# First panel by row parts, split-operand query jobs, and a new order of work in three mixers of a two-block transformer kernel

## What is computed

```python
# first block: three branches, then a mixture of experts
y_da  = diff_attention(da_q, da_k, da_v)        # 8 heads, x @ w_in gives all projections
y_ret = silu(r_g) * retention(r_q, r_k, r_v)    # 4 heads
y_mem = memory_attention(m_q, m_k, m_v)
merged = sum(gates * (branches @ w_branch));  x = layer_norm(alpha * x + merged @ w_o)
x = layer_norm(alpha * x + hier_moe(x))
# second model, layer 0: pool mixer and windowed attention ("second mixer"), dense ffn
z = h @ w_in;  ya = pool_mixer(p);  yb = windowed_gqa(q, k, v, sink)
y = concat(ya, yb) @ w_out
# layer 1: spatial gating ("third mixer"), mixture of experts
z = gelu(h @ w_in);  u, v = split(z)
v = layer_norm_2(v, sg_ln_g, sg_ln_b)
sv = einsum('gts,bnsgc->bntgc', w_s, v) + b_s
y = (u * sv) @ w_out
```

## Time and profile before

| | us |
|---|---|
| median of 3 executions (2126.43 to 2129.2) | 2126.73 |
| the profiled execution, its own time | 2135.3 |
| its span, first to last instruction | 2133.5 |
| PE busy | 2075.2 (97%) |
| DVE busy | 1727.4 (81%) |
| ACT busy | 1380.5 (65%) |
| chain that ended last: PE | 83% of the span |
| chain: DVE, DMA | 9%, 5% |

### The profile page before, as it was taken

How to read it: one execution, slowest core, us unless ns; L and a number is a source line. 1 busy time by engine, 2 the same in 40 slices (tenths; PEclk the granted TensorE clock), 3 DMA queues, 4 the chain that set the end, 5 groups by cost and what they waited for, 6 DMA issues and landing times.

```text
span 2133.5 us, 27437 instructions
## 1 busy us (share of the span) xinstructions
PE 2075.2 (97%) x10952; PEld 1767.2 (83%) x10952; DVE 1727.4 (81%) x2153; ACT 1380.5 (65%) x1702; POOL 47.7 (2%) x66
## 2 busy tenths in 40 slices
PE   7999999999999998999899999999999999999997
PEld 7889999987888777888688888888888888888886
DVE  2786778779898875766656999999999998999898
ACT  2566255557777653543544787877878787777774
POOL 0000000000000000000000000000000000000000
PEclk9999999999999999999999999999999999999999
DMA  8854797669999850765714999999999999999994
GB/s 303 316 224 171 303 372 272 218 228 378 380 374 389 330 198 3 275 246 228 276 40 183 380 389 380 382 368 392 365 387 372 388 376 376 380 376 385 388 407 163
DMA packets 60668, 659.24 MB, mean 309 GB/s; under 512 B 6384, under 2 KB 12400, under 8 KB 19312
## 3 DMA queue, kind: packets, MB, share of 16 engines
q1 hardware_dynamic: 48384, 597.84, 71.8%
q0 software_dynamic: 8736, 50.34, 6.2%
q10 hardware_dynamic: 3408, 9.18, 1.2%
HBM read 645.79 MB, written 11.53 MB: 308 GB/s over the span
## 4 chain that ended last, share of the span: by engine, by line
PE 83%; DVE 9%; DMA 5%; ACT 2%; issue 1%; DVEq 0%; ACTq 0%; SPq 0%
PE psum L2483 54%; PE psum L2219 14%; DVE stage_lo L1937 5%; DMA ring<-w_in 4%; PE psum L2197 4%; PE psum L2266 3%; PE psum L2643 1%; PE psum L2166 1%; PE psum L2256 1%; DMA mixer_tiles<-od_b_s_in 1%; ACT stage_hi L1397 0%; DMA arena<-x_in 0%; DVE h_lo L2107 0%; PE psum L2452 0%; PE psum L2380 0%
## 5 line engine op out<-in xcount | busy, mean ns | idle before, releaser
L1937 DVE TENSOR_TENSOR stage_lo<-ring,stage_hi 128x1024 fp32r<-128x1024 f32 (+1 forms) x934 | 1091.1, 1215 | 99.9 <-ACT stage_hi L1397 90.1
L1397 ACT ACTIVATE stage_hi<-ring 128x1024 fp32r<-128x1024 f32 (+1 forms) x934 | 943.0, 1051 | 304.7 <-PE psum L2483 94.9
L2483 PE MATMUL psum<-stage_hi,x_hi 128*128 128x512 f32 (+1 forms) x1344 | 528.9, 394 | 2.7 <-DVE stage_lo L1937 1.8
L2483 PE MATMUL psum<-stage_hi,x_lo 128*128 128x512 f32 (+1 forms) x1344 | 521.1, 388 | 0.0
L2483 PE MATMUL psum<-stage_lo,x_hi 128*128 128x512 f32 (+1 forms) x1344 | 519.9, 387 | 0.0
L2483 PEld LDWEIGHTS psum<-stage_hi,x_hi 128*128 128x128 f32 x1344 | 252.5, 188 | 53.5 <-DVE stage_lo L1937 3.1
L2483 PEld LDWEIGHTS psum<-stage_hi,x_lo 128*128 128x128 f32 x1344 | 252.3, 188 | 53.1
L2483 PEld LDWEIGHTS psum<-stage_lo,x_hi 128*128 128x128 f32 x1344 | 252.8, 188 | 49.1
L2219 PE MATMUL psum<-mixer_split 128*128 128x256 f32 x1344 | 259.8, 288 | 7.9 <-DVE mixer_split L1699 5.8
L2483 PE MATMUL psum<-stage_hi,h_hi 128*128 128x512 f32 x664 | 261.2, 393 | 5.0 <-DVE h_lo L2107 5.0
L2483 PE MATMUL psum<-stage_lo,h_hi 128*128 128x512 f32 x664 | 258.7, 390 | 0.0
(11 more groups left out here) (279 smaller groups left out, 1906.5 us busy)
## 6 DMA issues: line engine op xcount, KB each, us to landing
ring<-moe_w_gate_in SPq DMA_DIRECT2D x56, 2048.0 KB, 10.0
ring<-moe_w_up_in SPq DMA_DIRECT2D x56, 2048.0 KB, 10.0
ring<-moe_w_down_in SPq DMA_DIRECT2D x56, 2048.0 KB, 9.9
ring<-w_in SPq DMA_DIRECT2D x48, 2048.0 KB, 10.4
ring<-w_in_in SPq DMA_DIRECT2D x16, 2048.0 KB, 10.0
arena<-ada_w_in POOLq DMA_DIRECT2D x18, 1024.0 KB, 7.8
mixer_tiles<-ada_w_in POOLq DMA_DIRECT2D x16, 1024.0 KB, 7.9
ring<-ada_w_in SPq DMA_DIRECT2D x5, 2048.0 KB, 9.4
```

The source lines that it names most:

```text
L1397: act.activation(chunk_view(stage_hi, f, side, p, c), chunk_source(f, side, p, c), ACT.Copy)\
L1937: dve.tensor_tensor(chunk_view(stage_lo, f, side, p, c), chunk_source(f, side, p, c), chunk_view(stage_hi, f, side, p, c).bitcast(F32), AL ...
L2483: ins = pe.matmul(dst, a, b, start=start, stop=stop)
```

## The change

It has four parts. **Start:** the first panel comes in four parts by rows of the weights (two of the eight k blocks each), x in four parts beside them, each with a semaphore of its own; the x split goes first in the list; `da_q` 0 stays in full float32 and waits part by part, `da_q` 1 to 3 become split jobs. **Retention:** a fill job now stands ahead of `ret_out`, none after `ret_turn`, and the last `da_norm` follows the first `ret_out`. **Second mixer:** two exponent tiles (the second in `zeros`), two sums and two sink terms; the pool fills stand between `gqa_turn` and `gqa_out` of heads 3, 5, 6 and 7; the lo halves of the pool part come at the end. **Third mixer:** v is only centred and scaled; gain and shift go into the eviction of `gate_s`, with `sg_shift` = b_s + shift x the row sums of w_s, which two new matmuls against ones (`sum_gates`) and eight DVE instructions (`sg_bias`) make; `gate_s` moves between the `od_u` jobs; two loads of 512 KB are dropped and two (the last layer norm's rows) go from ACT's queue to the end of SP's.

```diff
-SPLIT = ("da_k", "da_v", ...
+SPLIT = ("da_q", "da_k", "da_v", ...
+GQA_FILL = {3: ("pool", 0, 0), 5: ("pool", 1, 0), 6: ("pool_map", 0, 0), 7: ("pool_map", 1, 0)}
...
-    s = gemms("da_q", 0) + splits("x", 0, 1, 2, 3) + gemms("da_q", 1, 2, 3) + gemms("da_k", 0, 1) + ada(0)
+    s = splits("x", 0, 1, 2, 3) + [("stage", "da_q", 1)] + gemms("da_q", 0, 1, 2, 3) + gemms("da_k", 0, 1) + ada(0)
...
-    s += [("ret_score", 0, 0), ("da_norm", DA_H - 1, 0)]
+    s += [("ret_score", 0, 0)]
     for h in range(RET_H):
-        s += [("ret_out", h, 0), ("ret_out", h, 1)] + (splits("x_late", 0, 1, 2, 3) if h == RET_H - 1 else [])
+        s += [fill.pop(0), ("ret_out", h, 0), ("ret_out", h, 1)] + ([] if h else [("da_norm", DA_H - 1, 0)])
+        s += splits("x_late", 0, 1, 2, 3) if h == RET_H - 1 else []
         s += [fill.pop(0)] + ada(6 + h) + ([("ret_score", h + 1, 0)] if h + 1 < RET_H else [])
-        s += [("ret_turn", h, 0), fill.pop(0)]
+        s += [("ret_turn", h, 0)]
...
-        s += [("gqa_out", h, 0)] + fill[:1]
-        del fill[:1]
+        s += [GQA_FILL[h]] if h in GQA_FILL else []
+        s += [("gqa_out", h, 0)]
...
-    s += [("gemm", "od_u", 1), ("stage", "od_u", 3), ("gemm", "od_u", 2), ("stage", "od_o", 0), ("gemm", "od_u", 3)]
-    s += [("gate_s", 0, 0), ("gate_s", 1, 0), ("split", "mix3", 0), ("gate_s", 2, 0), ("split", "mix3", 1)]
-    s += [("gate_s", 3, 0), ("split", "mix3", 2), ("split", "mix3", 3)]
+    s += [("stage", "od_u", 2), ("gemm", "od_u", 1), ("gate_s", 0, 0), ("gate_s", 1, 0), ("stage", "od_u", 3)]
+    s += [("sg_gate", 0, 0), ("split", "mix3", 0), ("sg_gate", 1, 0), ("split", "mix3", 1)]
+    s += [("gemm", "od_u", 2), ("gate_s", 2, 0), ("gate_s", 3, 0), ("stage", "od_o", 0)]
+    s += [("sg_gate", 2, 0), ("split", "mix3", 2), ("gemm", "od_u", 3), ("sg_gate", 3, 0), ("split", "mix3", 3)]
...
+            sp.dma_start(slot(first_panel[0], KT)[:, 2 * c:2 * c + 2, :].rearrange("p k n -> p (k n)"),
+                         first_panel[2][:, 2 * c * PANEL:2 * (c + 1) * PANEL]).then_inc(told, 16)
+            sp.dma_start(xT[:, 2 * c:2 * c + 2, :].rearrange("p k t -> p (k t)"),
+                         w["x"][0][:, 2 * c * T:2 * (c + 1) * T]).then_inc(x_in[c], 16)
...
-                    if a:
-                        act.wait_ge(gqa_probs, a)
+                    if a == 1:
+                        act.wait_ge(zeroed, 4 * 16)
+                    if a > 1:
+                        act.wait_ge(gqa_probs, a - 1)
...
+                elif kind == "sg_bias":
+                    dve.wait_ge(small_in, 4 * 16)
+                    dve.wait_ge(ws_summed, 1)
+                    for g in range(SG_G):
+                        b = job_bank(("gemm", "od_v", 2 + g // 4))
+                        ins = dve.scalar_tensor_tensor(sg_shift[:, g, :], bank(b, 4, P)[:, g % 4, :], col_a("sg_b", g),
+                                                       bs_rows[:, g, :], ALU.mult, ALU.add)
...
-                    settle(dve.tensor_tensor(v_tok, v_tok, over(sg_rows[:, 0, :], TB), ALU.mult))
-                    dve.tensor_tensor(v_tok, v_tok, over(sg_rows[:, 1, :], TB), ALU.add).then_inc(v_normed, 1)
...
+        def sum_gates():
+            for half in range(2):
+                evacuated(("turn_ws", half, 0))
+                s = ("gemm", "od_v", 2 + half)
+                pe.wait_ge(bank_free[job_bank(s)], index[s] // BANKS)
+                ins = pe.matmul(bank(job_bank(s)), ones, region(R_K + half * PANEL, PANEL), start=True, stop=True)
+            ins.then_inc(ws_summed, 1)
```

More of the change, by code:

```diff
@@ L114, in shape_constants @@
     return out
-SPLIT = ("da_k", "da_v", "m_q", "gate1", "m_k", "m_v", "branch1", "gate2", "branch2", "w_o")
+SPLIT = ("da_q", "da_k", "da_v", "m_q", "gate1", "m_k", "m_v", "branch1", "gate2", "branch2", "w_o")
 TURNED = ("da_v", "r_v", "m_v", "ev_p", "od_v")
@@ L129 @@
 HEAD_CHUNKS = [[(job, c) for job in jobs for c in range(chunks_in(job))] for jobs in HEAD_FILL]
-SPLIT_OF = {"da_k": "x", "da_v": "x", "r_q": "x", "r_k": "x", "r_v": "x", "r_g": "x", "gate0": "x", "m_q": "x", "gate1": "x_late", "gate2": "x_late", "m_k": "mem", "m_v": "mem",
+SPLIT_OF = {"da_q": "x", "da_k": "x", "da_v": "x", "r_q": "x", "r_k": "x", "r_v": "x", "r_g": "x", "gate0": "x", "m_q": "x", "gate1": "x_late", "gate2": "x_late", "m_k": "mem", "m_v": "mem",
             "branch1": "yret", "branch2": "ymem", "w_o": "merged", "ev_q": "h1", "ev_p": "h1", "ev_o": "mix1",
@@ L603, in build @@
         for s in plan:
-            if s[0] in ("ada", "stage", "hi", "lo", "part", "split", "lam", "sg_norm", "ln_early", "gqa_exp",
+            if s[0] in ("ada", "stage", "hi", "lo", "part", "split", "lam", "sg_norm", "sg_bias", "sg_gate", "ln_early", "gqa_exp",
                         "gqa_norm"):
@@ L1026, in _ @@
                 unit_loads(f, n, f["main"], u)
+            if n == 2:
+                for m, name in enumerate(("ln_g_2", "ln_b_2")):
+                    sp.dma_start(out_rows[:, m, :], w[name][1, 1].partition_broadcast(P)).then_inc(rows_loaded, 16)
             if f["routed"]:
@@ L1138, in walk @@
                     at, fill = panel[("gemm", q[1], q[2] - q[2] % 2)]
+                    if s == ("stage", "da_q", 1):
+                        for n in range(3):
+                            act.wait_ge(first_in[n], 16)
                     act.wait_ge(slot_full[at], 16 * fill)
@@ L1677, in staged_low, with pool_low @@
                               ALU.subtract).then_inc(w_lo_set, 1)
+        def pool_low(a):
+            s = ("pool_map", a, 0)
+            b = full(s)
+            dve.wait_ge(mix_hi_set, mix_parts[s])
+            for k in range(2):
+                n = 2 * a + k
+                ins = dve.scalar_tensor_tensor(mix1_lo[:, n, :], bank(b, 2, T)[:, k, :], col_a("pool_scale", n),
+                                               mix1_hi[:, n, :].bitcast(F32), ALU.mult, ALU.subtract)
+            ins.then_inc(bank_free[b], 1)
         def head_low(a):
@@ L1868, in walk @@
-                    dve.tensor_tensor(mix[:, 2 * a:2 * a + 2, :], mix[:, 2 * a:2 * a + 2, :], e2,
+                    if a == 0:
+                        dve.wait_ge(sg_shifted, 1)
+                    for k in range(2):
+                        g = 2 * a + k
+                        ins = dve.scalar_tensor_tensor(sg_v[:, g, :].rearrange("p (c t) -> p c t", t=P),
+                                                       bank(b, 4, P)[:, 2 * k:2 * k + 2, :], col_a("sg_g", g),
+                                                       over(sg_shift[:, g, :], 2), ALU.mult, ALU.add)
@@ L2184, in split_product @@
                 nxt = ("gemm", a, i + 1)
+                if s == ("gemm", "od_v", 2):
+                    pe.wait_ge(sg_shifted, 1)
                 if 0 in parts:
@@ L2239, in walk @@
                     if i == 0:
-                        if a == "da_q":
-                            pe.wait_ge(x_in, 16)
-                        elif a == "branch0":
+                        if a == "branch0":
                             evacuated(("da_out", DA_H - 1, 0))
@@ L2245, in walk @@
                                 evacuated(("da_out", n, 0))
-                    in_parts = a == "da_q" and i < 2
+                    in_parts = a == "da_q"
                     if not in_parts:
@@ L2255, in walk @@
                                 pe.wait_ge(*h_in(3, k))
+                            if i == 0 and a == "od_v" and k == 6:
+                                sum_gates()
                             ins = pe.matmul(bank(b), rhs[:, k, i % 2 * P:(i % 2 + 1) * P], wt[:, k, :],
```

89 lines of the change are left out of this document (40 added, 49 removed).

## The result

| | before | after |
|---|---|---|
| median, us | 2126.64 (4 executions, 2126.43 to 2129.2) | 2114.51 (4, 2113.64 to 2116.49) |
| ratio after to before, 95% interval | | 0.9929, 0.9913 to 0.9945 |
| profiled execution, its own time, us | 2135.3 | 2115.2 |
| PE busy, us | 2075.2 | 2066.3 |
| mean granted clock | 0.993 | 0.997 |

The change makes the kernel faster, by 12.1 us in the medians. The forecast was 24.7 us, to 2102.0, and the range ended at 2110. The two profiled executions differ by 20.1 us, so two things have to be explained: why the profiled ones are 4.6 us short of the sum, and why the medians lie 8 us closer together than the profiled executions.

A forecast was written before the change was run, and what follows sets the result against it. TensorE, busy 97% of the span, was taken as the bound. Gains of 5.7 (start), 3.6 (retention), 7.7 (second mixer) and 7.7 (third mixer) sum to 24.7 us, taking the median from 2126.7 to 2102.0; range 2097 to 2110.

The forecast's parts named there:

- the last line of the sum: Whole kernel: 24.7 us off the profiled 2135.3 gives 2110.6; standing 8.6 above the median, so the median becomes 2102.0.
- (a) to (e): Rivals: first job stays slow 0.17; expert loads 0.10; one mixer's wait only moves 0.15; slower 0.03; nothing measurable 0.05.
- Start: First float32 jobs, `da_q`: split jobs and loading by parts gain 5.7 us, bounds 0.9 to 7; job 0 ends at 18.4.
- rival (a): Start: all ten matmuls after the last part run at the lower clock, job 0 ends at 21.3; time 2104.9, chance 0.17.
- Retention: First mixer's heads: fill ahead of `ret_out` gains 3.6 us, bounds 2.5 to 4.8, with a 1.1 us wait for the mask.
- rival (b): 480 to 745 us: first experts' loads take back the 9.3 us of start and retention; time 2111.3, chance 0.10.
- Second mixer: Eight heads take 23.1 us instead of 31.3 as ACT's copy no longer waits behind the exponent; 7.7 us gained.
- Its lower bound: Second mixer: 4.6 us gained if the waits stay and only half the clock's loss is had back.
- Third mixer: From `od_u` 1 to `od_o` 0: net 7.7 us gained, bounds 4.5 to 9, after 1.7 for two added matmuls.

The follow-up runs named there:

- e1: The kernel before run again with no edit: median 2130.72 us over 12 executions, ratio to before 0.9998; its profiled execution took 2127.6 us.
- e6: The changed kernel with 20 more always-met waits at the start of TensorE's program: median 2110.86 us, ratio to before 0.9918.
- e10: The kernel before with 99 more always-met waits at the start of TensorE's program: median 2135.5 us, ratio to before 1.0026.
- e12: The kernel before with only the start changed, plus 20 always-met waits on TensorE: median 2126.14 us, ratio to before 0.9979.
- e11: The kernel before with only the second mixer's fill order changed, still one exponent tile: median 2124.93 us, ratio to before 0.9973.
- e14: The kernel before with only the second mixer's exponent a head ahead (two tiles), old fill order: median 2125.78 us, ratio to before 0.9989.
- e3: The kernel before with only the second mixer's part of the change: median 2124.2 us over 12 executions, ratio to before 0.9966.
- e7: The changed kernel with the start of before, the other three parts kept: median 2115.74 us, ratio to before 0.9935.

## Why the prediction was wrong, point by point

**The step that failed first** is the last line of the sum: "it stands 8.6 above the median, so the median goes from 2126.7 to 2102.0". It takes 24.7 us off the median, while part of those 24.7 stood in that one execution alone. A time that the change removes can't be removed twice. The nine executions of the changed kernel lie within 3.7 us, at granted clocks of 0.996 to 0.998, so the sum should have ended at the profiled one's 2110.6 for both. The measured profiled time is 2115.2, its median 2114.5. Of the 12.5 us by which the forecast missed, this step is 7.9 (8.6 put between the two, 0.7 measured). e1 shows the execution to be one of before's longer ones, and 7.1 of the 7.8 us between the two to lie where the change works. The 8.6 itself was partly too large: against the later medians of before, 2127.9 to 2130.9, that execution stands out by 4.4 to 7.4.

**The second miss, 3.4 us,** had no term at all: added instructions on TensorE, 99 of them, move the code behind a branch. e6, e10 and e12 show it. With the stop comes the lower clock: of the 3.4, 1.1 are the 16 turns alone. None of the forecast's rivals named it; (a) to (e) spoke of clock, loads and DVE's pace.

**Start:** first matmul at 5.67 and the last part at 14.4, the end of job 0 at 18.76 against 18.4, 5.1 us against 5.7. The size was right, in part by luck. TensorE's first matmuls in after:

```profile
5.67 2.04 PE L2305 MATMUL psum<-arena,ring 128*128 128x256 f32 x4 [5.67 <-DMA arena<-x_in]
10.65 8.45 PE L2305 MATMUL psum<-arena,ring 128*128 128x256 f32 x28 [2.94 <-DMA arena<-x_in]
```

The stretch from the landing of the last part to the end of job 0:

```profile
14.50:18.76 4.26, 4.21 (x21) 3.75 (x21) 3.05 (x3) 2.46 (x3) 0.00 (x0) 1.00 1.06 439
```

That is 0.20 us a record, the upper level, so rival (a) did not come about. Two misses cancelled here: the last part landed 1.5 us later than the forecast's 12.9 (0.5 of it because 4096 KB were counted as 4.0 MB and not as 4.2), and the ten matmuls behind it took 4.3 us, all at the upper level, where three slow ones and seven fast had been put at 5.5. And 5.1 is measured against an x that landed at 10.77; against e1's 9.70 it is 3.2.

**Retention:** the wait for the mask came as forecast (0.95 against 1.1), and at the start of `gate1` 0 the lead had grown by 3.45 against 3.6. Then 1.1 went to the lo halves of `gate1` 1, behind the `ada` panel. The forecast had followed DVE's order to the second head only.

**Expert loads,** rival (b): the lead fell from 7.2 to 5.6 near 520 us and came back to 7.5. Nothing was swallowed.

**Second mixer:** 23.36 us against 23.1 at a clock of 1.00, 8.5 gained against 7.7. The size was right in the profiled pair; over many executions it is 7.2. The reason was mostly wrong: the forecast named both edits, but held the exponent for what kept ACT's copy back; by e11 and e14 it is mostly the empty place between turn and `out`. Its lower bound does not follow from its terms either: 4.6 are the waits, so that "the waits stay and only half the clock's loss is had back" would have left 1.8.

**Third mixer:** 8.1 against 7.7, and 8.5 by itself. The steps came as forecast, first the row sums in `od_v` 0, then the one wait in `od_o` 0, 1.27 against 1.3:

```profile
1047.69 1.88 PE L2258 MATMUL psum<-arena 128*128 128x512 f32 x4
...
1099.16 2.06 PE L2248 MATMUL psum<-mixer_split 128*128 128x256 f32 x15 [1.27 <-DVE mixer_split L1719]
```

The two added matmuls are four records, 1.7 us from start to start (1047.69 to 1049.41), as forecast.

**What stays open:** whether before's first four executions, 2126.4 to 2129.2, were short by chance or by the chip; later ones had medians of 2127.9 to 2130.9. With it stays open how the 7.9 us divide between a long profiled execution and a short first median. By both ratios the change is worth some 15 us, by the first medians 12. Retention's 2 us of the trace could not be found in the times.

## What to carry to other kernels

Don't carry a sum made on one profiled execution over to the median by subtracting its distance: ask first whether the excess lies in the very stretches that the change removes, and profile the kernel before a second time. Where a program branches, count the instructions that a change adds ahead of the target, and look for an "issue" wait a few instructions behind it; a few met waits at an idle place are a cheap remedy. A copy between two steps of one engine was hidden more by work put between those steps than by freeing the engine that copies: of 5.3 us of waits the one left 0.4, the other 3.4.

## What the runs showed of the hardware that was not expected

- A second stop of 2.3 to 2.8 us, four matmuls behind a taken branch, that comes and goes with 99 or 20 instructions far ahead of it, and with it one more packet of 16384 bytes on the queue that brings code (92 against 91).
- TensorE fell to half clock behind one wait of 1.46 us and stayed at full clock behind another of 1.46 and then 1.74, in two executions of the same program. The kernel with such waits spread over 7.2 us in 9 executions, the one without them over 3.7 in 9; with the second mixer's waits alone gone (e3) it is 5.2 in 12 executions against 8.9 in e1's 12.
- Behind the two stops the granted clock is 0.66 over ten us, and 16 turns take 3.30 us instead of 2.24; behind the one stop of e7 they take 3.09, behind the one of before 2.24.
